# The last layer norm of an encoder step: VectorE and ScalarE share the row work, the shift is written to HBM ahead, and the rows are added to it by accumulating DMAs

## The chip, the cores and the metric

One NeuronCore of one Trainium2 chip runs the whole program. The metric is the device time of one execution in microseconds, lower is better. All data are float32; the matrix products are done with each operand split into a high and a low part.

## The reference, cut to what matters

One layer of a streaming encoder: 512 new rows (`x_prompt`) and 64 running rows (`x_sample`), 576 rows of 2048 in all. The change touches only how the last `_layer_norm` leaves the chip.

```python
def _layer_norm(x, g, b):
    xf = x.astype(jnp.float32)
    mu = jnp.mean(xf, -1, keepdims=True)
    var = jnp.mean(jnp.square(xf - mu), -1, keepdims=True)
    return ((xf - mu) * lax.rsqrt(var + LN_EPS) * g + b).astype(x.dtype)

def _finish_layer(x, y_a, y_b, y_c, g_mix, w_out, ln1_g, ln1_b, w_up, w_down, ln2_g, ln2_b):
    y = jnp.concatenate([_rms_norm(y_a, ...), _rms_norm(y_b, ...), _rms_norm(y_c, ...)], axis=-1)
    x = _layer_norm(ALPHA * x + jnp.einsum('btm,md->btd', y, w_out), ln1_g, ln1_b)
    hdn = jnp.square(jax.nn.relu(jnp.einsum('btd,df->btf', x, w_up)))
    return _layer_norm(ALPHA * x + jnp.einsum('btf,fd->btd', hdn, w_down), ln2_g, ln2_b)
```

The outputs of this norm are `y_prompt` (512 x 2048) and `y_sample` (64 x 2048). Before them the layer projects its input, runs a gated linear recurrence (RG-LRU) on 1024 of the columns, with two 128x128 gate weights `w_ra` and `w_rx` for each block of 128 channels, and two kinds of attention; these also write caches and states, which the change leaves alone.

## The kernel before

The program is written engine by engine (`block.sync`, `block.scalar`, `block.vector`, `block.gpsimd`, `block.tensor`), each a list of instructions in a fixed order with semaphores between them, so nothing is scheduled: an engine that waits holds back all that stands behind it in its own list. The 576 rows are held transposed, in two halves of 288 columns (`HALF`); half 1 is finished first.

**Weights.** SP loads the weights as 1 MB tiles (`raw`, 128 partitions x 8 x 256), in runs of 1 KB. ScalarE copies a tile to its high part `w_hi` (`hi`, L436), VectorE subtracts to get the low part `w_lo` (`lo`, L440), TensorE multiplies. A `raw` tile may be loaded anew when VectorE has made its low part.

**The gates.** At L925 to L937 ScalarE has finished the first group of projections, puts the forget gates' logs in SBUF (`logf_rows`) and stores them by two DMAs from its own queue. Then comes a loop over the eight channel blocks (L947 and on). Its first two instructions load `w_ra` and `w_rx` of the block (64 KB each) from ScalarE's queue. On TensorE each turn of the loop is half a group of projection products, then the gates' products (L2354), then the other half; ahead of the gates' products TensorE waits for both weights (`gw_in`) and for the convolution from VectorE.

**The end.** The last eight tiles of `w_down` (v = 0 to 7) are multiplied one after another. VectorE adds each product to `y` (L2083). TensorE transposes finished blocks of 256 columns of `y` to rows (`rows_transposed`, L2668, sixteen steps; steps 0 to 7 are half 1, steps 8 to 15 half 0), ScalarE copies each step out of PSUM to `y_rows` (`rows_copy`, L1381 and L1382) and VectorE takes its statistics (`row_stats`, L2053). `AFTER[v]` tells which steps follow tile v: 0, 1, 2 follow v = 0; 14 follows v = 7; 15 stands at the very end. A transposition of a later step waits until ScalarE has copied the step but one before it. A half has three row tiles t, of 128, 128 and 32 rows (`ROW_T`); `row_tile(h, t)` is `ROWS_1` for half 1, `ROWS_0` and `ROWC_0` ("y_rows_rest") for half 0. `row_means` makes mean and variance on VectorE (L2059), `row_sds` the root on ScalarE (L1387), `row_rstd` the reciprocal on VectorE (L2074). Then VectorE alone does the norm in two passes for each row tile:

```python
return dve.scalar_tensor_tensor(r, r, MV[0:w, 3 * h + t, 0:1], GR[0:w, :], ALU.subtract, ALU.mult)      # gain, L2065
return dve.scalar_tensor_tensor(r, r, RST[0:w, 3 * h + t:3 * h + t + 1], BR[0:w, c], ALU.mult, ALU.add)  # shift, L2069
```

`GR` and `BR` hold the gain and the shift of `ln2` repeated over 128 partitions; GpSimd loads each by a DMA of 1 MB (L2275, L2276) just before the last eight tiles, when the last accumulating DMAs of the down projection have been issued. For half 1 the passes stand between the tiles v = 3 to 6; for half 0 they are the end of the program. Finished rows are stored by plain DMAs: half 1 from GpSimd's queue (L2279 to L2284), half 0 from SP's (L849, L851), in five pieces. GpSimd also issues accumulating DMAs already, in the down projection: `add_rows` (L2241) adds 288 KB tiles to rows in HBM (`down_scratch`), in runs of 1152 bytes.

Of the kernel before, what the change touches and what calls it, by code (L numbers as in the profile page):

```python
# [79 lines left out]
def encoder_step(nc, x_prompt, x_sample, state_conv, state_lru, band_k, band_v, fox_k, fox_v, fox_logf,  # L80
# [5 lines left out]
    with ctx:  # L86
# [42 lines left out]
        r = Region()  # L129
# [49 lines left out]
        HE6, HB01, HE1 = (r.sb(f"h_{n}", [128, UK, HALF]) for n in ("e6", "b01", "e1"))  # L179
        r.close()  # L180
        r = Region()
        GR, BR = r.sb("ln2_g_rows", [128, D]), r.sb("ln2_b_rows", [128, D])
        r.close()
        r = Region()
        r.sb("y_hi_a", [128, NA * TOK])
# [164 lines left out]
        d_m0, d_ev = sem("down_first_tile"), [sem(f"down_added{m}") for m in range(2)]  # L350
        gb_in, rows_t, rows_c = sem("gain_shift_in"), sem("rows_t"), sem("rows_c")
        stats_done, row_sd, row_rs = sem("stats_done"), sem("row_sd"), sem("row_rstd")
        row_g, row_y, out_rows, out_rows_p = (sem(n) for n in ("row_gain", "row_y", "out_rows", "out_rows_first"))

        class Chain:

# [203 lines left out]
        def _(sp):  # L560
# [282 lines left out]
                sp.wait_ge(lo_done, N_E + v - 2 + 3)  # L843
                weights_e(v)

            for n in range(4):
                t, c = n // 2, slice(D // 2 * (n % 2), D // 2 * (n % 2 + 1))
                sp.wait_ge(row_y, 3 + n + 1)
                sp.dma_start(y_prompt[128 * t:128 * t + 128, c], ROWS_0[:, t, c]).then_inc(out_rows, 16)  # L849
            sp.wait_ge(row_y, 3 + 5)  # L850
            sp.dma_start(y_prompt[256:288, :], ROWC_0[:, :]).then_inc(out_rows, 16)  # L851

            sp.wait_ge(out_rows, 16 * 5)
            sp.wait_ge(out_rows_p, 16 * 4)
            sp.wait_ge(stores, 16 * 6)
            for p in range(2):
                sp.wait_ge(kv_out[p], 64 * 5)
# [3 lines left out]
        def _(act):  # L861
# [73 lines left out]
            act.activation(FQ[0:DEC, 4, :], PS[0:DEC, 7, 36:40], ACT.Copy).then_inc(ftc_done, 1)  # L935
            act.dma_start(p_fl.rearrange("(t p) h -> p t h", p=128), LFT[:, 0:4, :]).then_inc(stores, 16)
            act.dma_start(s_fl, LFT[0:DEC, 4, :]).then_inc(stores, 16)  # L937

            def stage(m, i):

# [443 lines left out]
            def row_sds(n, h):  # L1384
# [2 lines left out]
                act.activation(RST[:, 3 * h:3 * h + 2], MV[:, 3 * h:3 * h + 2, 1], ACT.Sqrt, bias=eps[:, :])  # L1387
                act.activation(RST[0:32, 3 * h + 2:3 * h + 3], MV[0:32, 3 * h + 2, 1:2], ACT.Sqrt, bias=eps[0:32, :]).then_inc(row_sd, 1)

            for v in range(8):  # L1390
                if v < 6:
                    hi_e(v + 2)
                if v == 3:
                    row_sds(1, 1)
                for s in AFTER[v]:
                    rows_copy(s)
            rows_copy(15)
            row_sds(2, 0)


        @block.vector
        def _(dve):
# [659 lines left out]

            def gain(h, t):
                w, r = ROW_T[t][1], row_tile(h, t)
                return dve.scalar_tensor_tensor(r, r, MV[0:w, 3 * h + t, 0:1], GR[0:w, :], ALU.subtract, ALU.mult)  # L2065

            def shift(h, t, c=slice(0, D)):
                w, r = ROW_T[t][1], row_tile(h, t)[:, c]
                return dve.scalar_tensor_tensor(r, r, RST[0:w, 3 * h + t:3 * h + t + 1], BR[0:w, c], ALU.mult, ALU.add)  # L2069

            def row_rstd(n, h):

# [5 lines left out]
            for v in range(8):  # L2078
                for m in range(2):
                    dve.wait_ge(*((unit_done, N_E + v + 3) if m else (d_m0, v + 1)))  # L2080
                    dve.wait_ge(y0_in[v % 4], 16)
                    at = Y0[:, tile_e(v) + m, :]
                    dve.tensor_tensor(at, at, PS[:, 2 * m + v % 2, 0:HALF], ALU.add if v < 4 else ALU.subtract).then_inc(d_ev[m], 1)  # L2083
                if v < 6:
                    lo_e(v + 2)
                for s in AFTER[v]:
                    row_stats(s)
                if v == 2:
                    row_means(1, 1)
                elif v == 3:  # L2090
                    row_rstd(1, 1)
                    dve.wait_ge(gb_in, 32)
                    chain(gain(1, 0))
                elif v == 4:
                    shift(1, 0).then_inc(row_y, 1)
                    chain(gain(1, 1))
                elif v == 5:
                    shift(1, 1).then_inc(row_y, 1)
                elif v == 6:
                    chain(gain(1, 2))  # L2100
                    shift(1, 2).then_inc(row_y, 1)
            row_stats(15)
            row_means(2, 0)
            gain(0, 0).then_inc(row_g, 1)
            row_rstd(2, 0)
            dve.wait_ge(row_g, 1)
            for t in range(2):
                for h in range(2):
                    shift(0, t, slice(D // 2 * h, D // 2 * (h + 1))).then_inc(row_y, 1)
                chain(gain(0, t + 1))  # L2110
            shift(0, 2).then_inc(row_y, 1)


        @block.gpsimd
        def _(pool):
# [157 lines left out]

            pool.wait_ge(combo, 4 * N_SUPER + 8)
            pool.dma_start(GR[:, :], ln2_g.to_broadcast([128, D])).then_inc(gb_in, 16)  # L2275
            pool.dma_start(BR[:, :], ln2_b.to_broadcast([128, D])).then_inc(gb_in, 16)  # L2276
            pool.wait_ge(gb_in, 32)
            pool.wait_ge(row_y, 1)
            pool.dma_start(y_prompt[288:416, :], ROWS_1[:, 0, :]).then_inc(out_rows_p, 16)  # L2279
            pool.wait_ge(row_y, 2)  # L2280
            pool.dma_start(y_prompt[416:512, :], ROWS_1[0:96, 1, :]).then_inc(out_rows_p, 16)
            pool.dma_start(y_sample[0:32, :], ROWS_1[96:128, 1, :]).then_inc(out_rows_p, 16)
            pool.wait_ge(row_y, 3)
            pool.dma_start(y_sample[32:64, :], ROWS_1[0:32, 2, :]).then_inc(out_rows_p, 16)  # L2284


        @block.tensor
# [434 lines left out]
```

## Time and profile before

| | us |
|---|---|
| median of 3 runs | 2359.68 (2357.44 to 2361.64) |
| the profiled execution | 2353.08 |
| its span, first to last instruction | 2351.3 |
| TensorE busy | 2294.7 (98%), mean granted clock 0.995 |
| VectorE busy | 1558.3 (66%) |
| ScalarE busy | 955.2 (41%) |
| GpSimd busy | 264.1 (11%) |
| moved by DMA | 421.99 MB, 179 GB/s over the span |

Starts and durations of single instructions are those of the profiled execution, which is 6.6 us (0.3%) under the median. 1.8 us of it lie outside the span. A DMA has two numbers: the issue, which is an instruction of an engine's queue (SPq, ACTq or GpSimd), and its time to landing, counted from the issue. The profile counts packets and the share of the 16 DMA engines' time that each queue took: q1 is SP's queue, q10 ScalarE's, q0 GpSimd's.

### The profile page before, as it was taken

To read this page: it belongs to the slowest core of one execution; us is meant where nothing else is said; L and a number is where in the kernel's file an instruction comes from. 1 tells how busy PE (TensorE), PEld (TensorE's weight loads), DVE (VectorE), ACT (ScalarE), POOL (GpSimd) and SP (SyncE) were. 2 spreads that over 40 slices of the span, in tenths; PEclk is the share of its full clock that TensorE was granted. 3 is DMA by queue.
4 is the path that set the end of the run, shared out by engine and by line. 5 is a ranking of instruction groups with operands and counts; after the bars stand their busy time and mean duration, and the time that the engine had idled before them with its cause. 6 is when DMAs were issued, how large, how long until landed. Compare 5 with 4: busy or idle time off the path is not lost. (4 is left out here: it accounts for less than half of the span.)

```text
span 2351.3 us, 39849 instructions
## 1 busy us (share of the span) xinstructions
PE 2294.7 (98%) x16967; PEld 2250.5 (96%) x16967; DVE 1558.3 (66%) x1181; ACT 955.2 (41%) x957; POOL 264.1 (11%) x296
## 2 busy tenths in 40 slices
PE   7999999999999999999999999999999999998986
PEld 7999999999888999999999999999999999998985
DVE  3311455533457676667777777778778778778868
ACT  3222344423445354654444444455245235234332
POOL 2010233300011202200000000002112112111100
PEclk9999999999999999999999999999999999999998
DMA  7264333344643567775445555579689689769873
GB/s 211 82 193 128 104 101 101 97 153 132 194 150 109 162 207 231 215 245 191 154 156 182 160 178 182 170 236 239 174 238 247 180 235 238 197 184 273 205 224 117
DMA packets 383510, 421.99 MB, mean 179 GB/s; under 512 B 13716, under 2 KB 359512, under 8 KB 382824
## 3 DMA queue, kind: packets, MB, share of 16 engines
q1 hardware_dynamic: 319936, 335.73, 45.4%
q0 software_dynamic: 27552, 48.17, 10.8%
q10 hardware_dynamic: 35912, 36.49, 4.5%
q8 instruction: 85, 1.39, 0.3%
q14 instruction: 25, 0.20, 0.0%
HBM read 339.47 MB, written 82.45 MB: 179 GB/s over the span
## 5 line engine op out<-in xcount | busy, mean ns | idle before, releaser
L2506 PE MATMUL psum<-x_e_hi,w_hi 128*128 128x288 f32 x1600 | 471.4, 295 | 8.6 <-DVE w_lo L1703 7.0
L2506 PE MATMUL psum<-x_e_lo,w_hi 128*128 128x288 f32 x1600 | 472.7, 295 | 0.0
L2506 PE MATMUL psum<-x_e_hi,w_lo 128*128 128x288 f32 x1600 | 472.2, 295 | 0.0
L2506 PE MATMUL psum<-x_b_hi,w_hi 128*128 128x288 f32 x1536 | 452.9, 295 | 6.8 <-DVE w_lo L1821 2.7
L2506 PE MATMUL psum<-x_b_lo,w_hi 128*128 128x288 f32 x1536 | 453.8, 295 | 0.0
L2506 PE MATMUL psum<-x_b_hi,w_lo 128*128 128x288 f32 x1536 | 453.5, 295 | 0.0
L440 DVE TENSOR_TENSOR w_lo<-raw,w_hi 128x2048 fp32r<-128x2048 f32 x64 | 152.4, 2382 | 277.1 <-ACT w_hi L436 276.5
L2506 PEld LDWEIGHTS psum<-x_e_hi,w_hi 128*128 128x128 f32 x1600 | 301.5, 188 | 10.5 <-DVE w_lo L1703 8.6
L2506 PEld LDWEIGHTS psum<-x_e_lo,w_hi 128*128 128x128 f32 x1600 | 301.4, 188 | 0.0
L2506 PEld LDWEIGHTS psum<-x_e_hi,w_lo 128*128 128x128 f32 x1600 | 301.4, 188 | 0.0
L2506 PEld LDWEIGHTS psum<-x_b_hi,w_hi 128*128 128x128 f32 x1536 | 289.5, 188 | 8.9 <-DVE w_lo L1821 3.5
L2506 PEld LDWEIGHTS psum<-x_b_lo,w_hi 128*128 128x128 f32 x1536 | 289.5, 188 | 0.1
L2506 PEld LDWEIGHTS psum<-x_b_hi,w_lo 128*128 128x128 f32 x1536 | 289.2, 188 | 0.0
L450 PE MATMUL psum<-x_hi,w_hi 128*128 128x288 f32 x1280 | 277.2, 298 | 3.1 <-DVE w_lo L440 3.1
L450 PE MATMUL psum<-x_lo,w_hi 128*128 128x288 f32 x1280 | 274.4, 295 | 0.0
L450 PE MATMUL psum<-x_hi,w_lo 128*128 128x288 f32 x1280 | 272.4, 294 | 0.0
L436 ACT ACTIVATE w_hi<-raw 128x2048 fp32r<-128x2048 f32 x64 | 122.5, 1914 | 231.7 <-PE psum L450 173.4
L450 PEld LDWEIGHTS psum<-x_hi,w_hi 128*128 128x128 f32 x1280 | 204.8, 188 | 5.6 <-DVE w_lo L440 3.3
L450 PEld LDWEIGHTS psum<-x_hi,w_lo 128*128 128x128 f32 x1280 | 205.5, 188 | 0.0
L450 PEld LDWEIGHTS psum<-x_lo,w_hi 128*128 128x128 f32 x1280 | 205.0, 188 | 0.0
L1244 ACT ACTIVATE w_hi<-sigma 128x2048 fp32r<-128x2048 f32 x55 | 105.7, 1922 | 227.1 <-PE psum L2506 211.1
L2506 PE MATMUL psum<-x_e,w_hi 128*128 128x288 f32 x896 | 182.0, 298 | 0.0
(390 smaller groups left out, 3786.4 us busy)
## 6 DMA issues: line engine op xcount, KB each, us to landing
raw<-in_w_down SPq DMA_DIRECT2D x62, 1024.0 KB, 7.1
raw<-in_w_up SPq DMA_DIRECT2D x54, 1024.0 KB, 6.6
raw<-in_w_in SPq DMA_DIRECT2D x40, 1024.0 KB, 5.3
a_even<-in_w_down SPq DMA_DIRECT2D x30, 1024.0 KB, 7.3
raw<-in_w_out SPq DMA_DIRECT2D x24, 1024.0 KB, 5.4
a_even<-in_w_up SPq DMA_DIRECT2D x24, 1024.0 KB, 6.7
h_scratch<-c_tile ACTq DMA_DIRECT2D x48, 288.0 KB, 2.8
down_scratch<-c_tile POOLq DMA_DIRECT2D x44, 288.0 KB, 5.7
```

Source lines behind the costliest of these rows:

```text
L436: act.activation(WH[s][:, :, :], RAW[s][:, :, :], ACT.Copy).then_inc(hi_done, 1)
L440: dve.tensor_tensor(WL[s][:, :, :], RAW[s][:, :, :], WH[s][:, :, :].bitcast(F32), ALU.subtract).then_inc(lo_done, 1)
L450: last_mm = pe.matmul(PS[:, 2 * to + h, 0:c], w, x[:, kk, HALF * h:HALF * h + c], start=(first and n == 0), stop=(final and n == 2))
L1244: act.activation(WH[par][:, :, :], src[:, :, :], ACT.Copy).then_inc(hi_done, 1)
L2506: mm = pe.matmul(PS[:, bank, 0:HALF], w, x[:, k, :], start=(k + n == 0), stop=(k == UK - 1 and n == 2))
```

## The change

Five things change, and no arithmetic but the order of the last addition.

- Ahead of the gate loop ScalarE's queue issues two DMAs from HBM to HBM that write the shift `ln2_b` into every row of `y_prompt` (4 MB) and `y_sample` (0.5 MB). They stand before the loads of `w_ra` and `w_rx` in that queue.
- `BR` and its load are gone.
- VectorE does only `gain` for each row tile. ScalarE does the multiplication by the reciprocal deviation (`scale`), as an `Identity` activation with a scale for each partition: for half 1 behind the copies of v = 5, 6 and 7, for half 0 at the end, in five pieces as before.
- All nine pieces of rows leave by accumulating DMAs, which add them to what stands in the outputs; all are issued by GpSimd, which first waits for the two shift DMAs.
- SP issues no output rows any more; it only waits for the nine.

```diff
@@ block.scalar, ahead of the gate loop
             act.dma_start(p_fl.rearrange("(t p) h -> p t h", p=128), LFT[:, 0:4, :]).then_inc(stores, 16)
             act.dma_start(s_fl, LFT[0:DEC, 4, :]).then_inc(stores, 16)
+            act.dma_start(y_prompt, ln2_b.to_broadcast([SEQ, D])).then_inc(shift_out, 16)
+            act.dma_start(y_sample, ln2_b.to_broadcast([DEC, D])).then_inc(shift_out, 16)
@@ block.scalar, the end
+            def scale(h, t, c=slice(0, D)):
+
+                act.wait_ge(row_rs, 2 - h)
+                act.wait_ge(row_g, 3 * (1 - h) + t + 1)
+                w, r = ROW_T[t][1], row_tile(h, t)[:, c]
+                act.activation(r, r, ACT.Identity, scale=RST[0:w, 3 * h + t:3 * h + t + 1]).then_inc(row_y, 1)
+
             for v in range(8):
...
                 for s in AFTER[v]:
                     rows_copy(s)
+                if v >= 5:
+                    scale(1, v - 5)
             rows_copy(15)
             row_sds(2, 0)
+            for t in range(2):
+                for n in range(2):
+                    scale(0, t, slice(D // 2 * n, D // 2 * (n + 1)))
+            scale(0, 2)
@@ block.vector, the end
-                    dve.wait_ge(gb_in, 32)
-                    chain(gain(1, 0))
-                elif v == 4:
-                    shift(1, 0).then_inc(row_y, 1)
-                    chain(gain(1, 1))
-                elif v == 5:
-                    shift(1, 1).then_inc(row_y, 1)
-                elif v == 6:
-                    chain(gain(1, 2))
-                    shift(1, 2).then_inc(row_y, 1)
+                    dve.wait_ge(gb_in, 16)
+                    gain(1, 0)
+                elif v in (4, 5):
+                    gain(1, v - 3)
             row_stats(15)
             row_means(2, 0)
-            gain(0, 0).then_inc(row_g, 1)
+            gain(0, 0)
             row_rstd(2, 0)
-            dve.wait_ge(row_g, 1)
-            for t in range(2):
-                for h in range(2):
-                    shift(0, t, slice(D // 2 * h, D // 2 * (h + 1))).then_inc(row_y, 1)
-                chain(gain(0, t + 1))
-            shift(0, 2).then_inc(row_y, 1)
+            gain(0, 1)
+            gain(0, 2)
@@ block.gpsimd, the end
             pool.dma_start(GR[:, :], ln2_g.to_broadcast([128, D])).then_inc(gb_in, 16)
-            pool.dma_start(BR[:, :], ln2_b.to_broadcast([128, D])).then_inc(gb_in, 16)
-            pool.wait_ge(gb_in, 32)
...
+            pool.wait_ge(shift_out, 32)
+
+            def add_out_rows(h, t, n, dst, p0=0, p1=None, c=slice(0, D)):
+
+                p1 = ROW_T[t][1] if p1 is None else p1
+                pool.wait_ge(row_y, n)
+                pool.dma_start(dst[:, c], row_tile(h, t)[p0:p1, c], accum_op=ALU.add).then_inc(out_rows, 16)
+
+            add_out_rows(1, 0, 1, y_prompt[288:416, :])
+            add_out_rows(1, 1, 2, y_prompt[416:512, :], 0, 96)
+            add_out_rows(1, 1, 2, y_sample[0:32, :], 96, 128)
+            add_out_rows(1, 2, 3, y_sample[32:64, :])
+            for t in range(2):
+                for n in range(2):
+                    add_out_rows(0, t, 4 + 2 * t + n, y_prompt[128 * t:128 * t + 128, :], c=slice(D // 2 * n, D // 2 * (n + 1)))
+            add_out_rows(0, 2, 8, y_prompt[256:288, :])
```

How the instructions stand now, in the engines' own order. The lines of the changed file are five to nine off those of the kernel before, so both numbers stand in the rows. ScalarE ahead of the gate loop, before; `x2` and the like count instructions:

```order
L934 ACTIVATE f_rows<-psum 128x16
L935 ACTIVATE f_rows<-psum 64x4
L936 DMA out<-logf_rows 128x4x4
L937 DMA out<-logf_rows 64x4
L947 UNCONDITIONAL_BRANCH
L947 ISA
L948 DMA w_ra<-in_w_rg_a 128x128
L949 DMA w_rx<-in_w_rg_x 128x128
```

The same place in the changed kernel:

```order
L928 ACTIVATE f_rows<-psum 64x4
L929 DMA out<-logf_rows 128x4x4
L930 DMA out<-logf_rows 64x4
L931 DMA out<-in_ln_b 512x2048
L932 DMA out<-in_ln_b 64x2048
L942 UNCONDITIONAL_BRANCH
L942 ISA
L943 DMA w_ra<-in_w_rg_a 128x128
L944 DMA w_rx<-in_w_rg_x 128x128
```

The two writes of the shift stand ahead of the gate weights in one queue. ScalarE at the end, from the copy of step 13 on, before:

```order
L1381 ACTIVATE y_rows<-psum 128x2x256
L1382 ACTIVATE y_rows_rest<-psum 32x256
L1381 ACTIVATE y_rows<-psum 128x2x256
L1382 ACTIVATE y_rows_rest<-psum 32x256
L1381 ACTIVATE y_rows<-psum 128x2x256
L1382 ACTIVATE y_rows_rest<-psum 32x256
L1387 ACTIVATE row_rstd<-row_mean_var,eps 128x2
L1388 ACTIVATE row_rstd<-row_mean_var,eps 32x1
```

The same place in the changed kernel:

```order
L1376 ACTIVATE y_rows<-psum 128x2x256
L1377 ACTIVATE y_rows_rest<-psum 32x256
L1390 ACTIVATE y_rows<-y_rows,row_rstd 128x2048
L1376 ACTIVATE y_rows<-psum 128x2x256
L1377 ACTIVATE y_rows_rest<-psum 32x256
L1390 ACTIVATE y_rows<-y_rows,row_rstd 32x2048
L1376 ACTIVATE y_rows<-psum 128x2x256
L1377 ACTIVATE y_rows_rest<-psum 32x256
L1382 ACTIVATE row_rstd<-row_mean_var,eps 128x2
L1383 ACTIVATE row_rstd<-row_mean_var,eps 32x1
L1390 ACTIVATE y_rows<-y_rows,row_rstd 128x1024 x4
L1390 ACTIVATE y_rows_rest<-y_rows_rest,row_rstd 32x2048
```

Scalings of half 1 stand between the last copies, and the five of half 0 behind the roots. VectorE at the end, from the last aggregation on, before:

```order
L2059 BN_AGGR row_mean_var<-row_stats 32x2
L2065 SCALAR_TENSOR_TENSOR y_rows<-y_rows,row_mean_var,ln_g_rows 128x2048
L2074 RECIPROCAL row_rstd<-row_rstd 128x2
L2075 RECIPROCAL row_rstd<-row_rstd 32x1
L2069 SCALAR_TENSOR_TENSOR y_rows<-y_rows,row_rstd,ln_b_rows 128x1024 x2
L2065 SCALAR_TENSOR_TENSOR y_rows<-y_rows,row_mean_var,ln_g_rows 128x2048
L2069 SCALAR_TENSOR_TENSOR y_rows<-y_rows,row_rstd,ln_b_rows 128x1024 x2
L2065 SCALAR_TENSOR_TENSOR y_rows_rest<-y_rows_rest,row_mean_var,ln_g_rows 32x2048
L2069 SCALAR_TENSOR_TENSOR y_rows_rest<-y_rows_rest,row_rstd,ln_b_rows 32x2048
```

The same place in the changed kernel:

```order
L2067 BN_AGGR row_mean_var<-row_stats 32x2
L2073 SCALAR_TENSOR_TENSOR y_rows<-y_rows,row_mean_var,ln_g_rows 128x2048
L2078 RECIPROCAL row_rstd<-row_rstd 128x2
L2079 RECIPROCAL row_rstd<-row_rstd 32x1
L2073 SCALAR_TENSOR_TENSOR y_rows<-y_rows,row_mean_var,ln_g_rows 128x2048
L2073 SCALAR_TENSOR_TENSOR y_rows_rest<-y_rows_rest,row_mean_var,ln_g_rows 32x2048
```

The five shift passes are gone from VectorE.

## Rows read from the trace of the kernel before

**Rows 1.** Chain that ended last, its last pieces: start, us, what.
```profile
2330.08 0.86 PE psum L2668 x6
2330.96 0.60 ACT y_rows L1381
...
2345.92 2.34 DVE y_rows_rest L2069
```
**Rows 2.** Instructions in order of time, the end: start, us, instruction, wait before it.
```profile
2327.49 0.60 ACT L1381 ACTIVATE y_rows<-psum 128x512 f32<-128x512 f32 x1 [6.15 <-PE psum L2668]
...
2329.13 0.80 DVE L2083 TENSOR_TENSOR y<-y,psum 128x288 f32<-128x288 f32 x2
...
2333.86 2.35 DVE L2065 SCALAR_TENSOR_TENSOR y_rows<-y_rows,row_mean_var,ln_g_rows 128x2048 f32<-128x2048 f32 x1
...
2336.38 2.48 DVE L2069 SCALAR_TENSOR_TENSOR y_rows<-y_rows,row_rstd,ln_b_rows 128x1024 f32<-128x1024 f32 x2
...
2348.29 0.34 SPq L851 DMA_DIRECT2D out<-y_rows_rest  x1
```
**Rows 3.** DMA view, 2348 to 2351.3: the last store and its time to landing.
```profile
out<-y_rows_rest SPq DMA_DIRECT2D x1, 256.0 KB, 2.6
```
**Rows 4.** Instructions in order of time, the first turn of the gate loop.
```profile
247.39 0.55 ACTq L937 DMA_DIRECT2D out<-logf_rows  x1
248.18 0.39 ACTq L948 DMA_DIRECT2D w_ra<-in_w_rg_a  x1
...
249.10 0.37 SPq L426 DMA_DIRECT2D raw<-in_w_in  x1
...
257.40 1.14 PE L2354 MATMUL psum<-xc,w_ra 128*128 128x290 f32 x4
...
257.61 1.91 ACT L436 ACTIVATE w_hi<-raw 128x2048 fp32r<-128x2048 f32 x1 [7.07 <-PE psum L450]
```
**Rows 5.** The line of the `w_ra` loads (L948), all eight.
```profile
DMA to landing us min/median/max: 1.9/2.0/3.2
```
**Rows 6.** DMA view, 44 to 50.5: copies of one HBM row to many.
```profile
q0 software_dynamic: 309, 1.51, 87.5%
...
rel_repeated<-rel_reversed_dram POOLq DMA_DIRECT2D x2, 384.0 KB, 6.8
```
**Rows 7.** DMA view, 2260.2 to 2264: the loads of gain and shift, and SP's.
```profile
q0 software_dynamic: 194, 1.46, 97.9%
q1 hardware_dynamic: 1, 0.00, 0.1%
...
raw<-in_w_down SPq DMA_DIRECT2D x1, 1024.0 KB, 9.7
```
**Rows 8.** TensorE and its clock by stretch: busy (instructions) of each engine, PEclk, DMA share, GB/s.
```profile
2260.00:2262.00 2.00, 1.82 (x10) 1.83 (x11) 1.97 (x4) 1.76 (x1) 0.00 (x0) 0.73 1.00 397
2262.00:2264.00 2.00, 2.00 (x10) 2.00 (x10) 2.00 (x2) 0.00 (x0) 0.00 (x0) 0.50 0.98 381
...
2266.00:2268.00 2.00, 2.00 (x17) 2.00 (x16) 1.28 (x2) 0.00 (x0) 0.00 (x0) 1.00 1.08 367
```
**Rows 9.** Instructions in order of time, tiles v = 0 and v = 1 of the end.
```profile
2269.89 1.91 ACT L1359 ACTIVATE w_hi<-raw 128x2048 fp32r<-128x2048 f32 x1 [8.13 <-DMA raw<-in_w_down]
...
2272.59 0.87 PE L2668 MATMUL psum<-ident,y 128*128 128x128 f32 x6 [2.95 <-ACT y_rows L1382]
...
2282.61 0.88 PE L2668 MATMUL psum<-ident,y 128*128 128x128 f32 x6 [1.49 <-ACT y_rows L1382]
```
**Rows 10.** DMA view, 2229.5 to 2233: accumulating DMAs alone.
```profile
q0 software_dynamic: 431, 0.48, 107.9%
```
**Rows 11.** DMA view, 253 to 256: a weight load alone.
```profile
q1 hardware_dynamic: 788, 0.79, 75.3%
```
**Rows 12.** DMA view, 2337 to 2342: two stores of half 0, 4 KB runs.
```profile
q1 hardware_dynamic: 288, 1.05, 51.3%
```
**Rows 13.** DMA view, 2227.5 to 2233: an accumulating DMA, time to landing.
```profile
down_scratch<-c_tile POOLq DMA_DIRECT2D x1, 288.0 KB, 4.8
```

More of the change, by code:

```diff
@@ L181, in encoder_step @@
         r = Region()
-        GR, BR = r.sb("ln2_g_rows", [128, D]), r.sb("ln2_b_rows", [128, D])
+        GR = r.sb("ln2_g_rows", [128, D])
         r.close()
@@ L352, in encoder_step @@
         stats_done, row_sd, row_rs = sem("stats_done"), sem("row_sd"), sem("row_rstd")
-        row_g, row_y, out_rows, out_rows_p = (sem(n) for n in ("row_gain", "row_y", "out_rows", "out_rows_first"))
+        row_g, row_y, out_rows = (sem(n) for n in ("row_gain", "row_y", "out_rows"))
+        shift_out = sem("row_shift_out")
         class Chain:
@@ L844, in _ @@
                 weights_e(v)
[L846 to L854, printed above, removed]
+            sp.wait_ge(out_rows, 16 * 9)
             sp.wait_ge(stores, 16 * 6)
@@ L2064, in gain @@
                 w, r = ROW_T[t][1], row_tile(h, t)
[L2065 to L2069, printed above, removed]
+                dve.scalar_tensor_tensor(r, r, MV[0:w, 3 * h + t, 0:1], GR[0:w, :], ALU.subtract, ALU.mult).then_inc(row_g, 1)
             def row_rstd(n, h):
@@ L2275, in _ @@
             pool.dma_start(GR[:, :], ln2_g.to_broadcast([128, D])).then_inc(gb_in, 16)
-            pool.dma_start(BR[:, :], ln2_b.to_broadcast([128, D])).then_inc(gb_in, 16)
-            pool.wait_ge(gb_in, 32)
[L2278 to L2284, printed above, removed]
+            pool.wait_ge(shift_out, 32)
[11 more added lines that the diff above has]
+            add_out_rows(0, 2, 8, y_prompt[256:288, :])
         @block.tensor
```

## Prediction, made before the changed kernel was run

> **What bounds the kernel now.** The page comes first: TensorE is busy for 98% of the span, so whatever holds TensorE up is paid in full, and whatever runs on another engine beside it is free. The second view is the chain that ended last. It leaves TensorE at the last transposition (2330.1) and from then on is one copy by ScalarE and VectorE's work up to 2348.26 [rows 1]; the last store is issued at 2348.29 and lands 2.6 us later, at 2350.9 [rows 2, 3]. So there are two places where this change can move the end: the tail of some 20 us after TensorE's last work, and any point earlier where TensorE is made to wait. The third view is the timeline around the place where the shift is now written, at 248 us. There the reader is to see the loads of the gate weights in ScalarE's queue at 248.18 and TensorE's use of them at 257.40 [rows 4].
>
> **Early: the shift written to the outputs.** ScalarE's queue is free for it at 247.39 + 0.55 = 247.9 [rows 4]; I put the issue at 248.0. It moves 576 rows of 8 KB, 4.72 MB. The two gate weights (0.13 MB) stand behind it in the same queue. A 64 KB weight load lands 2.0 us after its issue, which is nearly all start and receipt [rows 5]; I charge these 2.0 us once.
>
> How fast a row in HBM is copied to many rows in HBM is shown once in this trace: 309 packets took 87.5% of 16 engines for 6.5 us, 91 engine-us for 1.51 MB, so 16.6 KB/us for an engine and 265 KB/us for all [rows 6]. By that 4.72 MB take 17.8 us. The other end is the copy of one HBM row to 128 partitions of SBUF in runs of 8 KB: 0.979 x 3.8 x 16 = 59.5 engine-us for 1.46 MB, 393 KB/us, by which it takes 12.0 us [rows 7]. I take 17.8, because it is the row of the same kind (HBM to HBM). Gate weights: 0.13 MB / 265 = 0.5 us. They land at 248.0 + 2.0 + 17.8 + 0.5 = 268.3 (other end: 262.5). TensorE needs them at 257.40: it stalls 10.9 us (other end 5.1). Queued behind its wait are the gates' products, then the second half of the group, and all of TensorE's later work; nothing later gives the time back, since the loads and engines behind it are all released by TensorE's own progress.
>
> The 1 MB weight tile that SP issues at 249.10 [rows 4] will be late too, by about as much. ScalarE takes it at 257.61 before. In the new order it lands a few us after the gate weights, ScalarE and VectorE need some 2 us each for it, and TensorE has the gates' products and the group's second half to do first, 48 products of both halves of the columns; these hide it, and I charge nothing. If that cover were gone it would cost those few us.
>
> After a long stall the clock is low. Before, after an idle gap of 2.4 us, two stretches of 2 us hold 10 products each at a granted clock of 0.73 and 0.50 (0.50 is 1.2 GHz), where 17 are done at 1.00 (2.4 GHz) [rows 8]: 14 products of 0.118 us missing, 1.65 us. I add it once, as the stall here is longer; the bounds are 0 and 1.65.
>
> Early sum: 10.9 + 1.65 = **+12.5 us** (from 5.1 to 12.5).
>
> **Before the last tiles: one load less.** The tile of SP issued at 2260.15 took 9.7 us to land, and for 3.8 us after its issue SP's queue moved one packet while GpSimd's loads of gain and shift took 97.9% of the engines [rows 7]. Without the 1 MB of the shift it lands 1.05 MB / 393 KB/us = 2.7 us sooner, at 2267.2. ScalarE started on it at 2269.89 after a wait for that DMA, copied the rows behind it, and TensorE waited 2.95 us for the copy; at the next tile, where no DMA was late, the same wait is 1.49 us, because ScalarE must wait for TensorE's own products in any case [rows 9]. What comes back is 2.95 - 1.49 = **-1.46 us**; the bounds are that and 0.
>
> **Under the last tiles.** VectorE loses three shift passes of half 1, and ScalarE gains three scalings of about 1.9 us (an activation of 128x2048 takes 1.91 us [rows 4]). VectorE's relief is under TensorE's products except at the last: there TensorE's last transpositions wait for VectorE's addition, which stood behind the passes of half 1 and came at 2329.13 [rows 2]. Now it comes as soon as the products end, some 2 us sooner. But ScalarE copies step 14 at 2327.49 (0.9 us with its small part), then scales the last row tile of half 1 until 2330.3, and only then copies step 15, at 2330.25 in place of 2330.96. So of some 2 us **0.7 remain**; the scaling that is moved to ScalarE is what is late next.
>
> **The tail.** From the copy of step 15 to the first gain pass it is 2.90 us, from there to the first reciprocal ready 2.52 us [rows 1, 2]: 2330.25 + 2.90 + 2.52 = 2335.67. ScalarE scales a piece of 128x1024 in 1.04 us (between 0.60 for 512 [rows 2] and 1.91 for 2048 columns [rows 4]), so the first accumulating DMA can be issued at 2336.7. VectorE's two other gain passes end at 2340.4, and the last scaling at 2342.3, where the rows were ready at 2348.26 before: 6.0 us sooner. That gain the engines give; the question is whether the DMAs take it.
>
> An accumulating DMA is dear. Alone, 431 packets of 1.1 KB took 107.9% of 16 engines for 3.5 us, 140 ns each [rows 10]; a plain packet of 1 KB takes 0.753 x 3 x 16 / 788 = 46 ns [rows 11], so adding costs 94 ns on top. A plain packet of 4 KB takes 0.513 x 5 x 16 us over 256 = 160 ns [rows 12]. The four large pieces are 32 packets of 4 KB for each engine, and the last piece counts as four more. The trace doesn't show how the surplus grows with size. If it is fixed, a packet is 254 ns and 36 take 9.1 us; if it grows with the bytes it is 94 x 4096/1114 = 346, a packet is 506 ns, and they take 18.2 us. No row is nearer to either, so I take the middle, 380 ns, 13.7 us. Start and receipt: 288 KB landed after 4.8 us [rows 13], of which 16 packets are 2.24, so 2.56. The end is 2336.7 + 2.56 + 13.7 = 2353.0 against 2350.9: **+2.1 us** (from -2.6 to +6.5). The queue, not the engines, ends the program then; the five pieces are ready by 2342.3 and wait for each other.
>
> The Trainium skill (Collectives: The Full Stack, The bandwidth ceiling: the fold count and why AG ≠ RS ≠ AR) says that an adding DMA isn't slow by the addition but by reading two sources. By that a packet of 4 KB would be 2 x 160 = 320 ns, the tail -0.1 us, and the whole 2370.7. The trace bears it out badly: at 1.1 KB the factor is 3, not 2.
>
> **The sum.** 10.9 + 1.65 - 1.46 + 2.1 = **+13.2 us**; the 0.7 us are in the tail's start. Against the profiled execution: 2353.1 + 13.2 = 2366.3. The median of the three runs is 6.6 us above that execution, so it stands at 2359.7 + 13.2 = **2372.9 us**, 0.56% slower.
>
> **Rivals.**
> *The shift's writing is hidden.* If the gate weights overtook it or the write was done by 257.40, the early term would be 0: -1.46 + 2.1 = +0.6, 2360.3, and with the cheap adding 2355.6, faster. For it the write must end within 6.9 us, at 684 KB/us; the fastest stretch here shows 393 [rows 7], and both loads stand behind it in one queue. 0.08.
> *Both bounds at their cheap end*: 5.1 + 1.65 - 1.46 - 2.6 = +2.7, 2362.4. It needs HBM to HBM copies in 8 KB runs to go at the rate of loads into SBUF, and a surplus that is fixed. 0.12.
> *The queues take turns.* In this trace SP's tile waited until GpSimd's queue was empty [rows 7]. If instead SP's 1 MB at 249.10 is served beside the shift, the gate weights come later by its 64 packets of 46 ns for each engine, 2.9 us: +16.1, 2375.8. The Trainium skill (DMA: Bandwidth & Descriptors, Queues, rings and completion order) says that an engine goes round the queues that have work, a packet of several descriptors at a time, which would make this the usual case. 0.12.
> *Adding grows with the bytes*: the tail is +6.5 in place of +2.1, in all +17.6, 2377.3. 0.13.
> The forecast holds 0.55.
>
> A measurement of this kernel can tell about 0.2% from no change, 4.7 us, so slower begins at 2364.4. The forecast, the turns and the dear adding lie above it: 0.80, and of the cheap case 0.02. Within 0.2%: the rest of the cheap case and most of the hidden one, 0.15; faster: 0.03. The range is 2363.5 to 2379.5: it leaves out the hidden case and part of the cheap one below, and above only the turns and the dear adding together.
>
> **What the changed profile would show.** At 257 a wait of TensorE of 5 to 14 us ahead of the gates' products, for the DMA of `w_rx`, with a landing of 14 to 20 us instead of 2 to 4, and a lower clock behind it; in the seven later turns nothing. At the first of the last tiles the wait of 2.95 us is 1.5. The copy of step 15 stands behind a scaling. VectorE ends some 8 us before the last landing, ScalarE 6 us sooner than rows were ready before, and GpSimd's queue is busy from the first accumulating DMA to the end. The prediction is wrong if the gate weights land in time, or if a packet of 4 KB is added in under 250 ns.

## The result, and the profile after

| | before | after |
|---|---|---|
| median of 5 runs, us | 2358.72 (2357.44 to 2361.64) | 2371.45 (2370.32 to 2374.80) |
| the profiled execution, us | 2353.08 | 2374.80 |
| its span, us | 2351.3 | 2373.0 |
| TensorE busy, us | 2294.7 | 2299.0 |

The changed kernel is slower by a ratio of 1.0055 (95% interval 1.0041 to 1.0069), 12.7 us. 2372.9 was predicted. The two profiled executions lie further apart, 21.7 us: the one of before is 5.6 us under its median, the one of after 3.4 us over its own.

**The early stall.** The view of waits, TensorE alone, after: line, releaser, us in total, times, longest.

```profile
PE psum L2355 <- DMA w_rx<-in_w_rg_x: 13.3, 1, 13.3
PE psum L2507 <- DVE w_lo L1711: 10.6, 12, 3.8
...
PE psum L2669 <- ACT y_rows L1377: 3.0, 2, 1.5
```

The first row is new and now the longest wait of TensorE in the kernel. The third stood at 4.4 us with a longest of 2.9 before, and a wait of 2.6 us for `y` (L2083) has gone. The timeline at the place, which answers to [rows 4]:

```profile
247.22 0.60 ACTq L931 DMA_DIRECT2D out<-in_ln_b  x1
...
248.75 0.38 ACTq L943 DMA_DIRECT2D w_ra<-in_w_rg_a  x1
...
249.23 2.06 ACTq L944 DMA_DIRECT2D w_rx<-in_w_rg_x  x1
...
270.15 2.30 PE L2355 MATMUL psum<-xc,w_ra 128*128 128x290 f32 x4 [13.34 <-DMA w_rx<-in_w_rg_x]
```

The weights are issued at 248.75 and 249.23 and the gates' products start at 270.15 instead of 257.40. They also go slowly: four of them take 2.30 us where they took 1.14 [rows 4]. Timeline by stretch, after, with the columns of [rows 8]:

```profile
257.00:270.00 13.00, 0.00 (x0) 0.00 (x0) 2.29 (x1) 1.76 (x1) 0.00 (x0) 0.69 0.94 318
270.00:272.00 2.00, 1.84 (x4) 1.41 (x5) 0.00 (x0) 0.00 (x0) 0.00 (x0) 0.50 0.93 304
272.00:274.00 2.00, 2.00 (x6) 1.42 (x5) 0.00 (x0) 0.00 (x0) 0.00 (x0) 0.50 0.05 17
274.00:276.00 2.00, 2.00 (x10) 1.86 (x10) 0.00 (x0) 1.35 (x2) 0.00 (x0) 0.58 0.00 0
276.00:278.00 2.00, 2.00 (x17) 2.00 (x16) 0.31 (x1) 2.00 (x4) 0.79 (x1) 1.00 0.00 0
```

The granted clock is 0.50, which is 1.2 GHz, through the first four us after the stall, 0.58 in the next two, and 1.00 (2.4 GHz) from 276 on. To weigh the whole stage I compare the start of the same two high-part copies of ScalarE in both traces, one ahead of the gates and the next one behind them. The first stands at 257.61 before [rows 4]; the next one before, then both after:

```profile
273.56 1.91 ACT L436 ACTIVATE w_hi<-raw 128x2048 fp32r<-128x2048 f32 x1 [0.65 <-ACT stage L943]
```

```profile
256.85 1.91 ACT L437 ACTIVATE w_hi<-raw 128x2048 fp32r<-128x2048 f32 x1 [4.08 <-PE psum L451]
...
289.06 1.92 ACT L437 ACTIVATE w_hi<-raw 128x2048 fp32r<-128x2048 f32 x1 [0.65 <-ACT stage L938]
```

The first copy comes 0.8 us earlier than before, the second 15.5 us later; the stage between them took 15.95 us and takes 32.21. So it costs 16.3 us in this execution: 13.3 of wait, and 3.0 of slow clock.

**The DMAs in that stage.** DMA view after, 247 to 270, then 250 to 253, then 255 to 261: queue, packets, MB, share of 16 engines; then issues with the time to landing.

```profile
q10 hardware_dynamic: 1504, 4.86, 59.5%
q1 hardware_dynamic: 1452, 1.47, 22.3%
...
out<-in_ln_b ACTq DMA_DIRECT2D x1, 4096.0 KB, 18.6
raw<-in_w_in SPq DMA_DIRECT2D x2, 1024.0 KB, 17.4
...
w_rx<-in_w_rg_x ACTq DMA_DIRECT2D x1, 64.0 KB, 20.8
```

```profile
q10 hardware_dynamic: 107, 0.88, 70.5%
```

```profile
q10 hardware_dynamic: 203, 1.66, 78.1%
q1 hardware_dynamic: 204, 0.21, 15.5%
```

Three things are to be seen. The copy of the shift (q10, ScalarE's queue) goes at 4.86 MB / (0.595 x 23 x 16 us) = 22.2 KB/us for an engine, 355 KB/us for all, not 265. SP's weight tiles (q1) are served beside it, packet for packet: 203 against 204 here, 196 against 198 from 261 to 266. By 270, when `w_rx` lands, 1.47 MB of SP's, parts of two tiles, have gone through, 0.223 x 23 = 5.1 us of all engines. And both start late: the copy, issued at 247.22, has its first packet at 250.9, 3.6 us on, and SP's tile, issued at 248.35, has none at all before 253. 3.6 us of start, 13.7 for ScalarE's queue (0.595 x 23) and 5.1 for SP's are 22.4, and from the first write's issue to the landing of `w_rx` at 270.0 it is 22.8.

**The end.** Timeline after, the last tile and the tail, which answers to [rows 2]:

```profile
2347.19 0.60 ACT L1376 ACTIVATE y_rows<-psum 128x512 f32<-128x512 f32 x1 [4.25 <-PE psum L2669]
...
2347.95 1.99 ACT L1390 ACTIVATE y_rows<-y_rows,row_rstd 32x2048 f32<-32x2048 f32 x1
2349.84 0.57 ACT L1376 ACTIVATE y_rows<-psum 128x512 f32<-128x512 f32 x1
...
2356.69 1.90 POOL L2276 DMA_DIRECT2D out<-y_rows  x2 [5.70 <-ACT y_rows L1390]
...
2359.94 2.00 ACT L1390 ACTIVATE y_rows_rest<-y_rows_rest,row_rstd 32x2048 f32<-32x2048 f32 x1
...
2362.23 0.78 POOL L2276 DMA_DIRECT2D out<-y_rows_rest  x1 [1.20 <-ACT y_rows_rest L1390]
```

The copy of step 14 starts 19.70 us later than before, so 19.70 is to be taken off when these are set beside [rows 2]. The copy of step 15 is at 2349.84, behind a scaling; less 19.70 that is 2330.14 against 2330.96, 0.8 us gained. The first accumulating DMA of half 0 is issued at 2336.99 on the old scale, and the rows are ready at 2361.94, 2342.24 on the old scale, 6.0 us sooner than 2348.26.

The DMA view after, 2361 to 2370, in which accumulating DMAs alone run, then the last one's time to landing:

```profile
q0 software_dynamic: 497, 1.90, 107.4%
...
out<-y_rows_rest POOLq DMA_DIRECT2D x1, 256.0 KB, 8.8
```

1.074 x 9 x 16 = 155 engine-us for 1.90 MB are 12.3 KB/us for an engine, 0.33 us for 4 KB. The last piece lands at 2362.23 + 8.8 = 2371.0, which is 2351.3 on the old scale, against 2350.9 [rows 3].

### The profile page after: what moved, and what is told of

It is laid out like the page before. It is cut to its first block and busy times, and to the rows that moved or that the text cites. A ratio compares the mean times of both kernels' runs of the same rounds, so it can differ in the third digit from the quotient of the medians.

```text
span 2373.0 us, 39857 instructions
## 1 busy us (share of the span) xinstructions
PE 2299.0 (97%) x16967; PEld 2252.9 (95%) x16967; DVE 1543.9 (65%) x1173; ACT 967.5 (41%) x965; POOL 269.2 (11%) x300
```

## Experiments

The kernel before was timed on the same chip in each group of runs: 2358.53 us (runs 1 to 4), 2357.86 (5 to 7), 2358.52 (8). Intervals are of the ratio to it. The theory: the whole loss is the stall at the gates, since the last norm alone comes out even. The rivals: the tail costs too, by the price of adding; and the stall isn't set by the place in ScalarE's queue but by the engines' bandwidth.

### 1. The kernel before, with the two writes of the shift alone

```diff
             act.dma_start(s_fl, LFT[0:DEC, 4, :]).then_inc(stores, 16)
+            act.dma_start(y_prompt, ln2_b.to_broadcast([SEQ, D])).then_inc(shift_out, 16)
+            act.dma_start(y_sample, ln2_b.to_broadcast([DEC, D])).then_inc(shift_out, 16)
```

> The kernel before, with only the two HBM-to-HBM writes of the shift added at the changed kernel's place, ahead of the gate weights in ScalarE's queue; the rows are stored plainly over them later, as before. Theory (the loss is TensorE's wait for the gate weights behind these writes, 13.3 us in the changed kernel's trace, and the low clock after it, 1.65 to 3 us): +15 to +16.5 us on the kernel before, about 2374, and a wait of about 13 us for w_rx in the trace. Rival (the loss of 12.7 us between the medians comes mostly from the accumulating DMAs at the end): within 2 us of the kernel before.

Measured: 2374.21 us (5 runs), ratio 1.0061 [1.0048, 1.0074], 15.7 us slower. View of waits, TensorE:

```profile
PE psum L2359 <- DMA w_rx<-in_w_rg_x: 13.5, 1, 13.5
```

With nothing else changed the wait is that of the changed kernel. The writes carry the whole loss. Whether the rest of the change gives some of it back, these intervals can't tell: they are 11.3 to 17.5 us here and 9.7 to 16.3 for the changed kernel.

### 2. The changed kernel, with the writes behind the first gate weights

```diff
-            act.dma_start(y_prompt, ln2_b.to_broadcast([SEQ, D])).then_inc(shift_out, 16)
-            act.dma_start(y_sample, ln2_b.to_broadcast([DEC, D])).then_inc(shift_out, 16)
@@ block.gpsimd, in the gate stage
+            pool.wait_ge(gw_in, 32)
+            pool.dma_start(y_prompt, ln2_b.to_broadcast([SEQ, D])).then_inc(shift_out, 16)
+            pool.dma_start(y_sample, ln2_b.to_broadcast([DEC, D])).then_inc(shift_out, 16)
```

> The changed kernel, but the shift writes are issued by GpSimd once the first pair of gate weights has landed (some 4 us later). Theory: TensorE doesn't wait at the gates, the changed kernel's loss is gone, and what is left is -1.5 us (one load less) and the tail (+0 to +2): 2357 to 2359.5. Rival (4.7 MB of writes hurt wherever they stand, by the weight tile that comes late beside them): a wait of several us at the second half of the group or the next turn, 2362 or more.

Measured: 2358.20 us (12 runs), ratio 0.9995 [0.9986, 1.0003]. The wait for `w_rx` is gone. DMA view, 247 to 275:

```profile
out<-in_ln_b POOLq DMA_DIRECT2D x1, 4096.0 KB, 16.4
raw<-in_w_in SPq DMA_DIRECT2D x2, 1024.0 KB, 9.7
...
w_rx<-in_w_rg_x ACTq DMA_DIRECT2D x2, 64.0 KB, 3.1
```

The same 4.7 MB move 5 us later and cost nothing. That SP's tiles take 9.7 us instead of 6.0 to land is hidden by TensorE's work. The place was the loss, not the bytes. And the rest of the change, without the stall, is even with the kernel before: -0.3 us (-3.3 to +0.7).

### 3. The kernel before, without the load of the shift

The last pass adds the gain's rows in place of the shift's.

```diff
-                return dve.scalar_tensor_tensor(r, r, RST[...], BR[0:w, c], ALU.mult, ALU.add)
+                return dve.scalar_tensor_tensor(r, r, RST[...], GR[0:w, c], ALU.mult, ALU.add)
...
-            pool.dma_start(BR[:, :], ln2_b.to_broadcast([128, D])).then_inc(gb_in, 16)
```

> The kernel before without the 1 MB load of the shift rows ahead of the last tiles; the shift pass adds the gain rows in its place, so the outputs' last addition is wrong. Theory: the weight tile of v = 2 lands some 2.7 us sooner, TensorE's wait at the third transposition falls from 2.95 to 1.5 us, -1.46 us in all, 2357.2. Rival (the wait is not that DMA's, or it comes back later): no difference in the trace at that place, 2358.7.

Measured: 2355.69 us (12 runs), ratio 0.9990 [0.9980, 1.0000]. View of waits, TensorE:

```profile
PE psum L2667 <- ACT y_rows L1382: 3.0, 2, 1.5
PE psum L2667 <- DVE y L2083: 2.6, 1, 2.6
```

The first wait falls from 4.4 to 3.0 us, the 1.46 of the forecast, and the second, which hangs on the shift passes, stays. The medians differ by 2.8 us; the interval, 0 to 4.7, holds both.

### 4. The changed kernel, with plain DMAs in place of accumulating ones

The shift is left out altogether.

```diff
-                pool.dma_start(dst[:, c], row_tile(h, t)[p0:p1, c], accum_op=ALU.add).then_inc(out_rows, 16)
+                pool.dma_start(dst[:, c], row_tile(h, t)[p0:p1, c]).then_inc(out_rows, 16)
```

> The changed kernel without the shift writes and with plain DMAs in place of the accumulating ones, from the same queue in the same order; the outputs lack the shift. Theory: what the engines save at the end now reaches the end. Rows are ready 6 us sooner than before, the last store lands about 3.5 us after, the load less gives 1.46: -6 to -7.5 us, 2351 to 2353, so that against the kernel with late shift writes the adding itself costs 5 to 8 us. Rival (the tail is bound by GpSimd's issues or by ScalarE, not by the adding): within 2 us of that kernel.

Measured: 2350.92 us (6 runs), ratio 0.9967 [0.9956, 0.9979]. DMA view, 2335 to 2356:

```profile
q0 software_dynamic: 624, 2.36, 30.5%
...
out<-y_rows POOLq DMA_DIRECT2D x4, 512.0 KB, 3.5
```

Adding costs 2358.20 - 2350.92 = 7.3 us against run 2 by the medians. The traces show 5.7 of them in the tail: from the copy of step 14 to the end of the span it is 25.9 us in run 2 and 20.1 in run 4 (23.8 in the kernel before). The plain rows go at 2.36 MB / (0.305 x 21 x 16 us) = 23.0 KB/us for an engine; adding, at 12.3, takes 1.9 times as long. The division of the norm between two engines is worth 2355.69 - 2350.92 = 4.8 us against run 3 (4.3 by the tails of the traces), and all of it and more is paid for the adding. Against the forecast's 6.0 us sooner rows, 1.6 are lost at the very end, which the three next lines show: DMA busy in 40 slices of the last 6 us of the span, for the changed kernel, run 4 and run 1.

```profile
DMA  9596989899969969995920000000000000000000
```

```profile
DMA  9999599998999659045940100000000000000000
```

```profile
DMA  9999200000000000000000000295059900000000
```

In the first two the last rows were issued by GpSimd, and from the last packet to the end of the span it is 2.8 us (19 slices of 0.15) and 2.6 us. In the third SP issued them, and it is 1.2 us.

### 5. The changed kernel, with the writes at the same moment from GpSimd's queue

```diff
+            pool.wait_ge(ftc_done, 2)
+            pool.dma_start(y_prompt, ln2_b.to_broadcast([SEQ, D])).then_inc(shift_out, 16)
+            pool.dma_start(y_sample, ln2_b.to_broadcast([DEC, D])).then_inc(shift_out, 16)
```

> The changed kernel with the two shift writes issued by GpSimd at the same moment (when the forget logs are out), so that they stand in another queue than the gate weights but run beside them. Theory (the wait comes from standing behind the writes in one queue; DMA engines take turns between queues, as SP's tile beside them showed in the changed kernel's trace): the gate weights land within 4 to 7 us, TensorE waits 0 to 1 us at the gates, 2357 to 2361. Rival (whatever is issued after the writes waits for them, in any queue, as SP's tile did before the last tiles of the kernel before): a landing of 13 us or more, a wait of 6 us or more, 2366 or more.

Measured: 2366.27 us (9 runs, 2362.14 to 2369.09), ratio 1.0034 [1.0024, 1.0044]. View of waits and DMA view, 247 to 270, then 252 to 257:

```profile
PE psum L2356 <- DMA w_rx<-in_w_rg_x: 3.8, 1, 3.8
```

```profile
w_rx<-in_w_rg_x ACTq DMA_DIRECT2D x1, 64.0 KB, 12.6
```

```profile
q0 software_dynamic: 200, 1.64, 85.1%
q1 hardware_dynamic: 140, 0.14, 9.5%
q10 hardware_dynamic: 196, 0.09, 6.8%
```

The truth lies between the two theories: the landing of 12.6 us and the wait of 3.8 fit neither, and the time is the rival's. A queue of its own spares the weights 8 us of the 20.8, but a load of 64 KB still takes 12.6 us, three to six times what it takes alone. The reason is in the last three lines: 196 packets of 0.5 KB get as many turns as 200 of 8 KB, and each turn of the copy lasts 0.851 x 5 x 16 / 200 = 0.34 us. So both bandwidth and place count. The profiled execution is the lowest of the nine; it lies 2.9 us over that of run 2, its median 8.1 over run 2's, and what the others paid more than this trace shows stays open.

ScalarE's two copies at the gates stand at 256.37 and 278.04 in this run: the stage takes 21.67 us in place of 15.95, 5.7 us more, 3.8 of wait and 1.9 of slow clock.

### 6. Run 2, with the last scaling of half 1 ahead of the last copies

```diff
-                if v >= 5:
-                    scale(1, v - 5)
+                for t in {5: (0,), 6: (1, 2)}.get(v, ()):
+                    scale(1, t)
```

> The kernel with the shift writes behind the first gate weights, and ScalarE's scaling of half 1's last row tile moved from behind the copy of step 14 to behind the copy of step 13, so that it no longer stands ahead of the copy of step 15. Theory (that scaling is what is late after TensorE's last transposition, and everything behind it, the queue of accumulating DMAs too, starts when that copy ends): 1.6 to 1.9 us less, 2356.5. Rival (the queue of accumulating DMAs is the bound by itself): less than 0.5 us.

Measured: 2355.82 us (11 runs), ratio 0.9989 [0.9980, 0.9998], 2.4 us under run 2; set each against the kernel before in its own group, it is 1.7. Timeline, ScalarE:

```profile
2329.45 0.60 ACT L1374 ACTIVATE y_rows<-psum 128x512 f32<-128x512 f32 x1 [2.35 <-PE psum L2670]
...
2330.28 0.60 ACT L1374 ACTIVATE y_rows<-psum 128x512 f32<-128x512 f32 x1
```

The copy of step 15 now follows that of step 14 by 0.83 us instead of 2.65. This shows the prediction's step "the scaling that is moved to ScalarE is what is late next": it held back the copy by 1.8 us. Not all of it reaches the end. Counted from the copy of step 14, the first accumulating DMA of half 0 is issued 1.6 us sooner than in run 2, but the last one lands 0.9 us sooner (23.0 against 23.9) and the span ends 0.8 us sooner. The rest goes into the queue of accumulating DMAs, so the rival is half right; the medians, with the two intervals overlapping, can't weigh the 0.8 against the 1.8.

### 7. Run 6, with one row tile of half 0 shifted by VectorE and stored plainly by SP

```diff
+            for n in range(2):
+                c = slice(D // 2 * n, D // 2 * (n + 1))
+                r = row_tile(0, 1)[:, c]
+                dve.scalar_tensor_tensor(r, r, RST[:, 1:2], BR[:, c], ALU.mult, ALU.add).then_inc(row_s, 1)
@@ block.sync
+                sp.dma_start(y_prompt[128:256, c], ROWS_0[:, 1, c]).then_inc(out_plain, 16)
@@ block.gpsimd, the load of the shift, now behind the tile v = 1
+            pool.wait_ge(unit_done, N_E + 1 + 3)
+            pool.dma_start(BR[:, :], ln2_b.to_broadcast([128, D])).then_inc(gb_in, 16)
```

> The same kernel, and half 0's rows shared out: tile 0 and the 32 rest rows are scaled by ScalarE and added by accumulating DMAs (1.25 MB in place of 2.25), tile 1 gets its shift pass on VectorE and is stored by plain DMAs from SP; the shift rows for it are loaded when the weight tiles leave the DMA engines idle, after tile v = 1. Theory (at the end the accumulating queue is the bound, about 0.33 us for 4 KB on an engine, and engines and queue can work side by side): the queue ends some 3 to 4 us sooner, and so do VectorE's passes; another 3 to 5 us less, 2352 to 2354. Rival (the added load or SP's stores beside the accumulating ones take it back): 2356 or more.

Measured: 2351.71 us (6 runs), ratio 0.9969 [0.9957, 0.9981]: 6.2 us under the kernel before, which the changed one was 12.7 over. DMA view, 2339 to 2352:

```profile
q0 software_dynamic: 336, 1.31, 60.3%
q1 hardware_dynamic: 288, 1.05, 19.9%
...
out<-y_rows POOLq DMA_DIRECT2D x2, 512.0 KB, 6.7
out<-y_rows SPq DMA_DIRECT2D x2, 512.0 KB, 7.1
```

Where adding bounds the tail, taking two of five pieces off it pays, 4.1 us against run 6 (3.8 by the tails of the traces). The plain stores pay for the company: 7.1 us to landing.

### 8. The changed kernel, with 256 of the 576 rows of shift ahead of the weights

```diff
+            act.dma_start(y_prompt[0:256, :], ln2_b.to_broadcast([256, D])).then_inc(shift_out, 16)
@@ block.gpsimd, in the gate stage
+            pool.wait_ge(gw_in, 32)
+            pool.dma_start(y_prompt[256:512, :], ln2_b.to_broadcast([256, D])).then_inc(shift_late, 16)
+            pool.dma_start(y_sample, ln2_b.to_broadcast([DEC, D])).then_inc(shift_late, 16)
```

> The changed kernel with only 256 of the 576 shift rows (2.1 MB) written ahead of the gate weights; the other 320 rows are written by GpSimd once the weights have landed. Theory (TensorE waits for the data in front of the weights, and the wait is only what sticks out over the 8 to 9 us that TensorE has until it needs them; in the changed kernel everything up to the weights, SP's two tiles too, moved at about 337 KB/us): the weights land after 248 + 2 + (2.1 + 0.13 + about 1) MB / 337 = 259 to 260, so a wait of 1 to 3.5 us instead of 13.3, and with it 1 to 3 us of low clock at most: 2359 to 2364. Rival (the stall is a fixed price of any HBM-to-HBM write in that queue): 8 us or more, 2368 or more.

Measured: 2365.59 us (6 runs, 2361.71 to 2368.24), ratio 1.0030 [1.0018, 1.0042]. View of waits, then DMA view, 247 to 270:

```profile
PE psum L2358 <- DMA w_rx<-in_w_rg_x: 3.5, 1, 3.5
```

```profile
out<-in_ln_b ACTq DMA_DIRECT2D x1, 2048.0 KB, 10.8
...
w_rx<-in_w_rg_x ACTq DMA_DIRECT2D x1, 64.0 KB, 11.6
```

The stall falls with the bytes ahead, from 13.3 to 3.5 us: 9.8 us for 2.62 MB, 267 KB/us. That is what TensorE sees as the rate of the queue, SP's turns included, and it is nearly the 265 that I took from [rows 6], for another reason. By the copies of ScalarE the stage costs 6.3 us here, 3.5 of wait and 2.8 of clock. The wait and the landing came out as this run's forecast had them. The median, 2365.59, lies above its 2364 and below the rival's 2368: the profiled execution is again the lowest, and what the others paid more is as open as in run 5.

## Why the prediction was right

Its time, 2372.9, is 1.5 us over the median, and the medians of the parts bear out its shape: the writes alone +15.7 us (run 1), everything else -0.3 (run 2). That the two do not add up to 12.7 exactly is within the intervals. The mechanism is the forecast one: TensorE waits for gate weights that stand behind the copy in one queue. That the number is so close is partly luck. By the traces the terms add up to 16.8 us and not to the forecast 13.2, and the medians lie 12.7 apart. The terms, one by one:

**The copy's rate, the turns and the start (10.9 us; measured 13.3).** From the issue to the landing of `w_rx` I had 20.3 us, and it was 22.8. One error stood against two. The copy goes at 355 KB/us and not at 265: with the gate weights it is 13.7 us instead of 18.3. But I took from [rows 7] that SP's tile would wait, and it takes turns, which costs 5.1 us up to the landing. And I charged 2.0 us for start and receipt, where the first packet alone came 3.6 us after the issue. The rival *the queues take turns* was the one with the right mechanism, and I had given it 0.12. The Trainium skill (DMA: Bandwidth & Descriptors, Queues, rings and completion order), by which an engine goes round the queues that have work, agrees here, 203 packets against 204. [Rows 7] show a stretch of 3.8 us without turns, 194 packets against 1. It need not speak against them, as it begins at the issue of SP's tile: in the changed kernel that tile had no packet for the first 4.7 us either, and then took turns. In the trace of before, 250 to 251.2, the tile issued at 249.10 with no big copy beside it had 28 packets through within 2.1 us:

```profile
q1 hardware_dynamic: 28, 0.03, 34.7%
```

So a DMA that was issued beside a busy queue started late in both places; why it did, no run tells. And I had missed a row for the turns in the trace of before. In its DMA view from 161 to 190 four accumulating DMAs of GpSimd, in runs of 2304 bytes, go beside SP's tiles:

```profile
q0 software_dynamic: 2059, 4.63, 85.9%
q1 hardware_dynamic: 1957, 1.98, 23.1%
```

Such a row as [rows 7] alone should not have carried the term.

**The clock (1.65; measured 3.0).** I took the loss after a gap of 2.4 us for that after one of 10. In the changed kernel the clock is at 0.50 through the eight products of the gates and beyond. By the copies of ScalarE the clock costs 3.0 us there behind a wait of 13.3, 1.7 in run 1 behind 13.5 (31.13 us for the stage), 2.8 in run 8 behind 3.5 and 1.9 in run 5 behind 3.8. The step that failed is "I add it once, as the stall here is longer": the bound of 1.65 was no bound, and the price, 1.7 to 3.0 us, doesn't follow the length of the stall.

**The late weight tile (0).** The number is right, the reading was not. The tile issued at 249.10 is not the one that ScalarE takes at 257.61: in the changed kernel ScalarE copies that one at 256.85 all the same, while the tile issued at 248.35 takes 22.5 us and lands at 270.9. It is the next copy, at 273.56 before and 289.06 after, that needs it. So the cover was some 18 us and not the gates' products, and no wait for it stands behind them.

**One load less (-1.46).** Right in the trace: the longest wait falls from 2.9 to 1.5 us in the changed kernel and in run 3.

**Under the last tiles (0.7).** Right: 0.8 us, and run 6 shows that the scaling ahead of the copy was what stood in the way of the rest, of which a part would have reached the end.

**The engines' part of the tail (6.0 us).** Right: 6.0 in the trace, with the first accumulating DMA at 2336.99 on the old scale against a forecast of 2336.7.

**The price of adding (0.38 us for 4 KB; measured 0.33).** Too dear: from the first issue to the last landing it is 14.3 us instead of 16.3. The middle of my two extrapolations from [rows 10] was the wrong step. The Trainium skill (Collectives: The Full Stack, The bandwidth ceiling: the fold count and why AG ≠ RS ≠ AR) has the adding in a collective bound by the reading of two sources. By it the sum had 320 ns; the trace agrees at 4 KB, with a factor of 1.9 between the changed kernel and run 4, where at 1.1 KB it was 3. "No row is nearer to either" was wrong: the row of the accumulating DMAs from 161 to 190, shown above, gives 0.859 x 29 x 16 / 2059 = 194 ns for 2.2 KB. Carried on in a line from 140 ns at 1.1 KB [rows 10] it makes 281 at 4 KB, so my dear end of 506 had a row against it.

**The last landing to the end (not in the sum; 1.6 us).** I treated the end of the program as the last landing, since that was so with SP's stores. With GpSimd's it is 1.6 us later, as run 4 showed. It took away most of the 2.0 us that the cheaper adding gave, and so the tail came out as forecast, +0.4 + 1.6 = 2.0 against 2.1, by two errors.

**What the profile should show.** A wait of 5 to 14 us, a landing of 14 to 20, a wait of 1.5 in place of 2.95: they are there, with 13.3, 20.8 (just over the range) and 1.5. "VectorE ends some 8 us before the last landing" was a slip against my own numbers, which made 12.6; VectorE's last pass ends at 2359.9, and it is 2371.0 - 2359.9 = 11.1.

Of the profiled executions' 21.7 us these terms explain 16.3 - 1.5 + 0.4 + 1.6 = 16.8, less the 0.8 us by which this one was ahead at 247. The other 5.7 came between 280 and 2225 us (of before), where the same 14283 instructions of TensorE take that much longer. 3.4 of it is idle time of TensorE, in waits for `w_lo` (L1711: 10.6 us in 12 waits, 7.0 in 6 before). 2.3 is longer busy time, which stays unexplained. Runs 1 to 8, with the same code there, have 7.4 to 9.5 us of these waits, so they vary from one execution to the next and aren't the change's. Why the medians are 12.7 apart and not 16.8 these traces, one for each kernel, can't settle: the interval reaches to 16.3.

## What to carry to other kernels

A write that nobody waits for still has a place in a queue, and its place is priced by what stands behind it: 4.7 MB ahead of two 64 KB weights cost 12 to 16 us, the same 4.7 MB behind them nothing. Moving an addition into the DMA pays only where the DMA engines have time for it: rows that are added take 1.9 times as long as rows that are stored, and at the end of a program that is bare. Divide such work by what bounds each part (run 7), not all one way.

## What the runs showed of the hardware

- Queues took turns packet by packet whatever their size: 196 packets of 0.5 KB beside 200 of 8 KB (run 5). A small load beside a copy in 8 KB runs is slowed by the copy's packets, to 12.6 us for 64 KB, even from a queue of its own.
- A tile's load issued just behind a 4.7 MB copy on another queue had no packet for 4.7 us, where one without it had 28 through within 2.1 us of its issue.
- A row in HBM was copied to many HBM rows at 22.2 KB/us for an engine in runs of 8 KB, against 16.6 in [rows 6].
- An accumulating DMA of 4 KB runs goes at 12.3 KB/us for an engine, a plain one from the same queue at 23.0.
- From the last packet to the end of the span it was 2.6 to 2.8 us where GpSimd had issued the last DMA, and 1.2 where SP had.
- A stall of TensorE of 3.5 to 13.3 us was followed by a stretch at a lower granted clock worth another 1.7 to 3.0 us, and the longer stalls did not pay the more: 1.7 and 3.0 behind 13.5 and 13.3, 1.9 and 2.8 behind 3.8 and 3.5.
